# A hybrid decoder step: x tiles of blocks three to five transposed by DMA instead of by TensorE

## The chip, the cores and the metric

The kernel runs on the 8 cores of one Trainium2 chip. Every core does the same work on its own data: one prompt sequence of 2048 rows and 16 running sequences of 4 rows (64 sample rows). The cores don't talk to each other. The metric is the device time of the slowest core, in microseconds (us). In the text PE is TensorE, DVE is VectorE, ACT is ScalarE, POOL is GpSimd, and SP is the sync engine, which here only issues DMAs.

## The reference

```python
mod = silu(c) @ w_ada + b_ada                      # (B, 3D), D = 1024
shift, scale, gate = split(mod, 3)
h = rms_norm(x, g_norm) * (1 + scale) + shift
p = h @ w_in                                       # [h_A | B_A | C_A | z_A | u_B | v_B | z_B], 3584 wide
s = C_A * h_A
y_A = B_A * dwconv3(s) * silu(z_A)                 # width 512; a running sequence starts from its conv buffer
v_n = layer_norm(v_B, g_v, b_v)
y_B = u_B * (tril(W_s) v_n + b_s) * silu(z_B)      # width 512, chunks of 128 positions, 8 heads
out = rms_norm(x + gate * ([y_A | y_B] @ w_out), g_final)
```

Besides `out` for prompt and samples the kernel returns the conv buffers left behind and the normalised v rows of the samples.

## The kernel before

**Blocks.** The 16 tiles of 128 prompt rows are worked through in five blocks of 4, 4, 3, 3 and 2 tiles. The third block also holds the 64 sample rows as a fourth tile. In the code they have the indices 0 to 4 (`B.i`). A block needs `hT`, the modulated x with the 1024 features on the partitions, as 8 slices k of [128, rows]. There are two such buffers, block b uses `hT[b % 2]`.

**Preparing a tile.** `prep_load` loads 128 rows of x into `xa`; for the later blocks there are two such buffers. `prep_sq` takes the sum of squares on ACT (L378) and the power -1/2 on POOL (L380, L382). `prep_xn` scales the rows on DVE into `xn`, in bf16 (L389); there are two `xn` buffers. `prep2` transposes the tile on PE, as eight transpositions of 128x128 into one PSUM bank (L403), and copies the bank into `hT` on ACT (L408) or DVE (L410). When all tiles of the next block are there, `prep3` applies scale and shift in place, one slice k at a time, on ACT (L419) and DVE (L423, and L434, L437 for the sample columns).

**Working a block.** `A1(B, j)` and `A2(B, j)`, for j = 0 to 3, make four projections of group A (L477 on PE, with ACT and DVE reading the banks). `V` makes the projection of v and its statistics. `GB(B, j)` makes two projections of group B, takes a silu on ACT (L644), multiplies on DVE (L647), does the spatial mix on PE (L656), adds the bias on DVE (L666) and multiplies on POOL (L676). Between the calls of `GB` stands the output stage of the block before: `C_mm` is the output projection (L704), `C_s1` multiplies by the gate (L720, L721) and adds x on DVE (L723), `C_sq` takes the sum of squares on ACT (L733), `C_s2` makes the factor (L791, L793), and `C_s3` scales on DVE (L802) and stores.

**Where the preparation stands.** For blocks one and two it is worked in with the start-up and with block one. For block three (`PB[2]`) it is spread over block two: scaling of tiles 0 and 1 at `V` (j = 2), their transpositions at j = 3, those of tiles 2 and 3 (the samples) in `GB(0)` and `GB(1)`. For blocks four and five the scaling of tile 0 stands in `GB(3)` two blocks ahead, and the transposition of tile j behind `A2(B, j)` of the block before.

**Order.** Each engine and each DMA queue runs its instructions in the order in which the Python code emits them. `Sched.op` collects what an instruction must wait for from the names of the buffers that it reads and writes. Same-engine waits between two PE instructions are left out, but one between two DMAs never is, even if both stand in the same queue:

```python
if (not d.is_dma) and (not dma) and d.eng == eng:
    if eng == "pe":
        continue
    ...
o.deps.append(d)
```

A waiting DMA holds all that stands behind it in its queue. SP's queue holds the xa loads of the later blocks, the xc loads (x again, for the residual), the gate copies and all stores. PSUM has 8 banks, given out in turn by `nbank()`; a matmul waits until the last readers of its bank are done.

Of the kernel before, what the change touches and what calls it, by code (L numbers as in the profile page):

```python
# [5 lines left out]
F32 = mybir.dt.float32  # L6
# [6 lines left out]
D = 1024  # L13
# [177 lines left out]
def build_nc(limit=None):  # L191
# [42 lines left out]
    wout_bf = A("wout_bf", [128, 2, 8, 512], BF16)  # L234
    hT = [A(f"hT{i}", [128, 8, 512], BF16) for i in range(2)]
    NXA = 2
    xa = [A(f"xa{i}", [128, D], F32) for i in range(NXA)]
    xn = [A(f"xn{i}", [128, D], BF16) for i in range(2)]
    junk = A("junk", [128, D], BF16)
    spad = [A(f"spad{j}", [128, 514], F32) for j in range(4)]  # L240
    ssamp = [A(f"ssamp{j}", [128, 16, 6], F32) for j in range(4)]
    gv_bc = A("gv_bc", [64, 512], F32)
    bv_bc = A("bv_bc", [64, 512], F32)
    gf_bc = A("gf_bc", [128, D], F32)
    gate_p = A("gate_p", [128, D], F32)
    gate_s = A("gate_s", [128, D], F32)
    bsT = A("bsT", [128, 4, 128], F32)
    bias2 = A("bias2", [128, 4, 128], F32)
    Wt = A("Wt", [128, 8, 128], BF16)
# [122 lines left out]
    def prep_sq(B, i):  # L372
        ti, P, kind = B.tiles[i]
        ra = pst[(B.i, i)]
        rn = nxt("xn", 2)
        st, sres = nstat()
        ss, rs = st[0:P, 0:1], st[0:P, 1:2]
        op("act", lambda e: e.activation(out=junk[0:P, :], in_=xa[ra][0:P, :], func=AF.Square, accum_out=ss),  # L378
           r=[("xa", ra)], w=[sres, "junk"])
        op("pool", lambda e: e.tensor_scalar(out=rs, in0=ss, scalar1=1.0 / D, scalar2=EPS, op0=ALU.mult, op1=ALU.add),  # L380
           r=[sres], w=[sres])
        op("pool", lambda e: e.tensor_tensor(out=rs, in0=rs, in1=mhalf[0:P, 0:1], op=ALU.pow),  # L382
           r=[sres, "mhalf"], w=[sres])
        pst[(B.i, i)] = (ra, rn, rs, sres)

    def prep_xn(B, i):
        ti, P, kind = B.tiles[i]
        ra, rn, rs, sres = pst[(B.i, i)]
        op("dve", lambda e: e.tensor_scalar(out=xn[rn][0:P, :], in0=xa[ra][0:P, :], scalar1=rs, scalar2=None,  # L389
                                            op0=ALU.mult),  # L390
           r=[("xa", ra), sres], w=[("xn", rn)])
        pst[(B.i, i)] = rn

    def prep2(B, i, eng):
        ti, P, kind = B.tiles[i]
# [186 lines left out]
    def V_group(B, kind, grp, mid):  # L582
# [35 lines left out]
        def scale_v():  # L618
            for q, (ti, _) in enumerate(grp):
                bk = bks[q]  # L620
                if kind == "p":
                    op("act", lambda e, bk=bk, ti=ti, q=q: e.activation(  # L622
                        out=vn_bf[ti][:, :], in_=bk.t[:, :], func=AF.Identity, bias=nm[:, q:q + 1], scale=rs[:, q:q + 1]),
                       r=[bk.res, sres], w=[("vn", ti)])
                    continue
                vz, vzr = ntmp()
                op("act", lambda e: e.activation(out=vz[0:P, :], in_=bk.t[0:P, :], func=AF.Identity, bias=nm, scale=rs),
                   r=[bk.res, sres], w=[vzr])
                op("act", lambda e: e.copy(out=vn_s[:, :], in_=vz[0:P, :]), r=[vzr], w=["vn_s"])
                op("pool", lambda e: e.tensor_tensor(out=vnS[:, :], in0=vz[0:P, :], in1=gv_bc[:, :], op=ALU.mult),  # L630
                   r=[vzr, "gv_bc"], w=["vnS"])
                op("pool", lambda e: e.tensor_tensor(out=vnS[:, :], in0=vnS[:, :], in1=bv_bc[:, :], op=ALU.add),
                   r=["vnS", "bv_bc"], w=["vnS"])
                store(nvs[:, :], vnS[:, :], ["vnS"], "out_nvs")
        return scale_v
# [303 lines left out]
    def late_loads_2(g):  # L939
        load("sp", gate_p[:], bada_g.partition_broadcast(128), "bg_p", g)  # L940
        load("sp", gf_bc[:], g_final.partition_broadcast(128), "gf_bc", g)
        load("sp", gv_bc[:], g_v.partition_broadcast(64), "gv_bc", g)
        load("sp", bv_bc[:], b_v.partition_broadcast(64), "bv_bc", g)

    nb = len(PB)
    cq = []

    def C_step(B, i, nload=None):
        C_mm(B, i, 0, 8)
        C_s1(B, i)  # L950
        cq.append((B, i))
        if nload is not None:
            C_load(*nload)
        if len(cq) >= 3:
            C_s3(*cq.pop(0))
        if len(cq) >= 2:
            C_s2(*cq[-2])
# [5 lines left out]
    for b in range(nb):  # L963
# [15 lines left out]
        for j in range(4):  # L979
            if not late:  # L980
                if j < 2:
                    nxp(prep_load, j + 2)
            A1(B, j)
            if b == 0 and j == 3:
                V2()
            if not late:
                nxp(prep_sq, j + 1)
            elif j == 3 and b == 1:
                nxp(prep_sq, 2)
                nxp(prep2, 0, "act")  # L990
            if j < 2 and cq and not last:
                C_s3(*cq.pop(0))
                if cq:
                    C_s2(*cq[0])
            A2(B, j)
            if last and j == 2 and cq:
                C_s3(*cq.pop(0))
                if cq:
                    C_s2(*cq[0])
            if not late:  # L1000
                nxp(prep2, j, "act")
                nxp(prep_xn, j + 1)
            if b == 0 and j == 0:
                late_loads_1([("spadB", 0)])
            if b == 1 and j == 0:
                wblk_ops()
            if j == 2 and b > 1:
                first_c()
            if b == 1 and j == 2:
                nxp(prep_sq, 0)  # L1010
                nxp(prep_sq, 1)
            if j == (1 if last else 2):
                V(B, (lambda: nxp(prep_xn, 0)) if b == 1 else None)
                if b > 0:
                    V2()
            if b == 0 and j == 2:
                wt_ops()
            if b == 0 and j == 3:
                nxp(prep_sq, 0)
                nxp(prep_sq, 1)  # L1020
                bias2_ops()
                nxp(prep_xn, 0)
                nxp(prep_xn, 1)
            if b == 1 and j == 2:
                nxp(prep_xn, 1)
                nxp(prep_load, 2)
                nxp(prep_load, 3)
            if b == 1 and j == 3:
                nxp(prep2, 1, "act")
                nxp(prep_xn, 2)  # L1030
        if not late and N2 is not None:
            for i in range(2):
# [10 lines left out]
        for j in range(4):  # L1043
# [18 lines left out]
            if b == 1 and j >= 2:  # L1062
                prep3(NX, range(4 * j - 8, 4 * j - 4), "both")
            if j == 3 and N2 is not None and b > 0:
                prep_xn(N2, 0)
            GB(B, j)
            if b == 0 and j == 1:
                nxp(prep2, 0, "act")
                nxp(prep2, 1, "dve")
# [6 lines left out]
                nxp(prep2, 3, "dve")  # L1076
                prep3(NX, range(8), "both")
            if b == 1 and j < 2:
                nxp(prep2, 2 + j, "act")
                if j == 0:  # L1080
                    nxp(prep_xn, 3)
                prep_load(N2, j)
# [4 lines left out]
        if b == 0:  # L1087
            for k in range(8):
                S.alias(("yT", 1, k), [("wada", 3), ("xa", 6), ("xa", 7)])
            late_loads_2([("win", 22, 0)])  # L1090
        if last:
            C_mm(B, 0, 0, 7)
            C_mm(B, 0, 7, 8)
# [68 lines left out]
```

How the kernel before makes its waits and increments, by code:

```python
        def run(e, eng):  # L113
            seen = {}
            nw = 0
            for o in streams[e]:
                need = {}
                waits = list(o.deps)
                if o.is_dma and o.prev is not None:
                    waits.append(o.prev)
                for d in waits:
                    key = d.sem.num
                    if key not in need or need[key][1] < d.val:
                        need[key] = (d.sem, d.val)
                for key, (sem, val) in need.items():
                    if seen.get(key, 0) >= val:
                        continue
                    eng.wait_ge(sem, val)
                    seen[key] = val
                    nw += 1
                ins = o.fn(eng)
                if o.is_dma:
                    ins.then_inc(o.sem, 16)
                elif o.needed:
                    ins.then_inc(o.sem, 1)
            stats[e] = (len(streams[e]), nw)
# [18 lines left out]
            @block.sync  # L155
            def _(eng):
                run("sp", eng)
                for q in self.QUEUES:
                    last = {}
                    for o in streams[q]:
                        if o.is_dma:
                            last[o.sem.num] = (o.sem, o.val)
                    for sem, val in last.values():
                        eng.wait_ge(sem, val)
```

## Time and profile before

| | |
|---|---|
| median of 3 runs | 343.68 us (343.39 to 365.61) |
| the profiled execution | 343.48 us |
| its span, first to last instruction, slowest core | 341.7 us |
| spans of the 8 cores | 338.1 to 341.7 us |
| busy in the span: PE, DVE, ACT, POOL | 287.9, 186.5, 122.0, 110.6 us |
| granted PE clock, mean of the core | 0.970 |

The profile is of one execution on the slowest core. A timeline row gives the start and the duration of a merged group of instructions, and in brackets how long its engine had been idle before it and what ended that. Matmuls are pipelined, so the duration of a group of them overlaps the next group; distances between starts tell what PE spends. Block two runs from about 104 to 169 us, block three to 231, block four to 284, block five to the end.

### The profile page before, as it was taken

The page shows a single profiled execution, that of the slowest core. Times are in us where ns is not written, and L with a number is a line of the kernel's source. Part 1 is how long each engine was busy: PE and PEld are TensorE (multiplying, and loading weights), DVE is VectorE, ACT ScalarE, POOL GpSimd, SP SyncE. Part 2 cuts the span into 40 slices and gives each one's busy share as a digit, 9 for nine tenths or more (in the row PEclk, how much of TensorE's full clock was granted, in tenths as well). Part 3 has the DMA queues.
Part 4 walks back from the last instruction along what each step waited for, and adds up shares of the span by engine and source line. Part 5 has one row for each costly group of instructions (what it writes and reads, how often), then busy time and mean ns, then how long its engine had stood idle before and what let it go on. Part 6 is the DMA issues. An engine that isn't in the chain of part 4 may idle for free.

```text
span 341.7 us, 5602 instructions; the slowest of 8 cores (338.1 to 341.7 us)
## 1 busy us (share of the span) xinstructions
PE 287.9 (84%) x1767; PEld 151.4 (44%) x1792; DVE 186.5 (55%) x350; ACT 122.0 (36%) x215; POOL 110.6 (32%) x161
## 2 busy tenths in 40 slices
PE   0324639997799999999999999999999999999840
PEld 0222324443444445444455454446555557765410
DVE  0321015444564454846778836468863666667982
ACT  2611024207452234723445262443415244232320
POOL 7293065214423431412226342121432112222210
PEclk9999959999999999999999999999999999999995
DMA  5999999999999973193122715111180102527223
GB/s 130 214 166 165 170 160 146 176 160 257 204 213 182 228 131 94 31 255 118 62 92 93 205 44 149 61 63 62 61 238 11 33 0 94 154 70 195 90 111 124
DMA packets 14157, 44.51 MB, mean 130 GB/s; under 512 B 1968, under 2 KB 2352, under 8 KB 13104
## 3 DMA queue, kind: packets, MB, share of 16 engines
q0 software_dynamic: 6624, 21.24, 34.7%
q1 hardware_dynamic: 7504, 22.91, 22.2%
q8 instruction: 15, 0.25, 0.3%
q14 instruction: 14, 0.11, 0.1%
HBM read 51.02 MB, written 8.85 MB: 175 GB/s over the span
## 4 chain that ended last, share of the span: by engine, by line
PE 54%; DMA 24%; DVE 9%; issue 6%; POOL 3%; ACT 2%; DVEq 1%; POOLq 0%; SPq 0%; ACTq 0%
PE pb L477 31%; PE pb L704 12%; DMA win_bf<-win_l 12%; DMA wada<-wada_l 10%; PE pb L592 7%; DMA xc<-x_p 2%; DVE ob L802 2%; PE pb L403 2%; PE pb L656 1%; PE pb L814 1%; POOL xa L314 1%; DVE ob L723 1%; DVE tmp L532 1%; DVE ob L720 1%; DVE ob L721 1%
## 5 line engine op out<-in xcount | busy, mean ns | idle before, releaser
L477 PE MATMUL pb<-hT,win_bf 128*128 128x512 bf16 (+3 forms) x672 | 125.6, 341 | 4.1 <-DVE hT L410 1.8
L477 PEld LDWEIGHTS pb<-hT,win_bf 128*128 128x128 bf16 x680 | 66.0, 98 | 59.1 <-issue 4.9
L704 PE MATMUL pb<-wout_bf,yT 128*128 128x512 bf16 (+1 forms) x246 | 56.8, 379 | 2.7 <-POOL yT L676 1.2
L477 PE MATMUL pb<-hT,wh 128*128 128x512 bf16 (+3 forms) x277 | 53.9, 355 | 3.6 <-ACT hT L419 3.6
L676 POOL TENSOR_TENSOR yT<-tmp,tmp 128x512 bf16<-128x512 f32 (+3 forms) x20 | 22.0, 1098 | 67.7 <-DVE tmp L666 37.0
L551 POOL TENSOR_TENSOR yT<-tmp,tmp 128x512 bf16<-128x512 f32 (+3 forms) x20 | 23.7, 1185 | 58.0 <-DVE tmp L546 41.1
L733 ACT ACTIVATE junk<-ob 128x1024 bf16<-128x1024 f32 (+1 forms) x16 | 16.9, 1057 | 71.5 <-DVE ob L723 58.7
L477 PEld LDWEIGHTS pb<-hT,wh 128*128 128x128 bf16 x280 | 27.7, 100 | 27.9 <-issue 7.9
L532 DVE SCALAR_TENSOR_TENSOR tmp<-spad,pv,tmp 128x512 f32<-128x512 f32 (+2 forms) x40 | 26.3, 658 | 20.3 <-ACT tmp L525 13.1
L704 PEld LDWEIGHTS pb<-wout_bf,yT 128*128 128x128 bf16 (+1 forms) x256 | 23.9, 98 | 29.3 <-issue 2.4
L592 PE MATMUL pb<-wv_bf,hT 128*128 128x512 bf16 (+1 forms) x133 | 29.6, 379 | 0.2
L419 ACT ACTIVATE hT<-hT,shT,aT 128x384 bf16<-128x384 bf16 (+2 forms) x28 | 18.0, 694 | 26.3 <-DVE aT L468 25.4
L525 ACT ACTIVATE tmp<-spad,pv 128x512 f32<-128x512 f32 (+2 forms) x20 | 12.7, 636 | 38.4 <-DVE spad L514 29.7
L389 DVE TENSOR_SCALAR xn<-xa,stat 128x1024 bf16<-128x1024 f32 (+1 forms) x17 | 12.8, 755 | 24.5 <-POOL stat L382 24.4
L403 PE MATMUL pb<-ident,xn 128*128 128x128 bf16 (+1 forms) x136 | 11.5, 238 | 16.9 <-DVE xn L389 16.9
L514 DVE TENSOR_TENSOR spad<-pb,tmp 128x512 f32<-128x512 f32 (+2 forms) x20 | 11.7, 585 | 22.5 <-PE pb L477 11.0
L647 DVE TENSOR_TENSOR tmp<-pb,tmp 128x512 f32<-128x512 f32 (+3 forms) x20 | 11.9, 595 | 19.7 <-ACT tmp L644 19.7
L802 DVE SCALAR_TENSOR_TENSOR ob<-ob,stat,gf_bc 128x1024 f32<-128x1024 f32 (+1 forms) x16 | 20.5, 1280 | 1.5 <-POOL stat L793 1.4
L723 DVE TENSOR_TENSOR ob<-ob,xc 128x1024 f32<-128x1024 f32 (+1 forms) x15 | 18.4, 1225 | 4.7 <-DMA xc<-x_p 2.4
L378 ACT ACTIVATE junk<-xa 128x1024 bf16<-128x1024 f32 (+1 forms) x17 | 17.9, 1053 | 7.4 <-DMA xa<-x_p 7.0
L592 PEld LDWEIGHTS pb<-wv_bf,hT 128*128 128x128 bf16 (+1 forms) x136 | 13.3, 99 | 15.6 <-issue 0.4
L622 ACT ACTIVATE vn_bf<-pb,stat 128x512 bf16<-128x512 f32 x16 | 11.2, 774 | 24.2 <-DVE stat L616 12.8
(88 smaller groups left out, 261.1 us busy)
## 6 DMA issues: line engine op xcount, KB each, us to landing
y_p<-ob SPq DMA_DIRECT2D x15, 512.0 KB, 2.7
xc<-x_p SPq DMA_DIRECT2D x14, 512.0 KB, 7.8
wada<-wada_l POOLq DMA_DIRECT2D x6, 1024.0 KB, 36.0
xa<-x_p POOLq DMA_DIRECT2D x10, 512.0 KB, 40.1
win_bf<-win_l POOLq DMA_DIRECT2D x17, 256.0 KB, 43.5
xa<-x_p SPq DMA_DIRECT2D x8, 512.0 KB, 6.6
wout_bf<-wout_l POOLq DMA_DIRECT2D x2, 1024.0 KB, 60.4
wh<-winh_l POOLq DMA_DIRECT2D x4, 256.0 KB, 27.5
```

The lines of the kernel that those rows point to most:

```text
L378: op("act", lambda e: e.activation(out=junk[0:P, :], in_=xa[ra][0:P, :], func=AF.Square, accum_out=ss), r=[("xa", ra)], w=[sres, "junk"])
L403: ii = pe.transpose(out=tv[:, k, 0:P], in_=xn[rn][0:P, k * 128:(k + 1) * 128], identity=ident[0:P, 0:P])
L419: op("act", lambda e, k=k: e.activation(out=hb[:, k, 0:B.NP], in_=hb[:, k, 0:B.NP], func=AF.Identity, scale=aT[:, k, 0:1], bias=shT[:, k, ...
L477: ii = pe.matmul(bk.t[:, 0:B.N], lhsT=wsl(m, k), rhs=hT[B.h][:, k, 0:B.N], start=(k == 0), stop=(k == 7))
L532: ii = e.scalar_tensor_tensor(out=o[:, 0:NP], in0=spad[j][:, tp:tp + NP], scalar=cw(j, tp), in1=a[:, 0:NP], op0=ALU.mult, op1=ALU.add)
L551: op("pool", lambda e: e.tensor_tensor(out=yT[B.y][:, j, 0:N], in0=c2[:, 0:N], in1=sg[:, 0:N], op=ALU.mult), r=[c2r, sgr], w=[("yT", B.y, j)])
L592: ii = pe.matmul(bk.t[0:P, :], lhsT=hT[B.h][:, k, ti * 128:ti * 128 + P], rhs=wv_bf[:, k, :], start=(k == 0), stop=(k == 7))
L676: op("pool", lambda e: e.tensor_tensor(out=yT[B.y][:, 4 + j, 0:N], in0=tU[:, 0:N], in1=mb[:, 0:N], op=ALU.mult), r=[tUr, mbr], w=[("yT", B ...
L704: ii = pe.matmul(bk.t[R, :], lhsT=yT[B.y][:, k, ti * 128:ti * 128 + P], rhs=wout_bf[:, n, k, :], start=(k == 0), stop=(k == 7))
L723: op("dve", lambda e: e.tensor_tensor(out=o[R, :], in0=o[R, :], in1=xt[R, :], op=ALU.add), r=[ores, xr], w=[ores])
L733: op("act", lambda e: e.activation(out=junk[R, :], in_=o[R, :], func=AF.Square, accum_out=st[R, 0:1]), r=[ores], w=[sres, "junk"])
L802: op("dve", lambda e: e.scalar_tensor_tensor(out=o[R, :], in0=o[R, :], scalar=rs, in1=gf_bc[R, :], op0=ALU.mult, op1=ALU.mult), r=[ores, s ...
```

## The change

Nine tiles, those of blocks three to five, are no longer transposed by PE and copied by ACT. `prep_xn` issues a transposing DMA on SP right behind the scaling, from `xn` into `hT`. Tile 0 of blocks four and five goes into a buffer that the current block is still reading; its DMA (`prep2d`) is issued behind the last `GB` of that block. There are four `xn` buffers instead of two. Room for them comes from `gv_bc` and `bv_bc`, which move into the partitions 0 to 63 of `gate_s`, of which only 64 to 127 were used. Apart from this, `C_sq` of the output stage is now emitted in the following `GB`, behind its silu on ACT, instead of directly behind `C_s1`; `flush` does that, and once more behind the last `GB`.

```diff
+    NXN = 4
-    xn = [A(f"xn{i}", [128, D], BF16) for i in range(2)]
+    xn = [A(f"xn{i}", [128, D], BF16) for i in range(NXN)]
-    gv_bc = A("gv_bc", [64, 512], F32)
-    bv_bc = A("bv_bc", [64, 512], F32)
+    gv_bc, bv_bc = gate_s[0:64, 0:512], gate_s[0:64, 512:1024]
...
-    def prep_xn(B, i):
+    def prep_xn(B, i, now=True):
...
         pst[(B.i, i)] = rn
+        if B.i > 1 and now:
+            prep2d(B, i)
+
+    def prep2d(B, i):
+        ti, P, kind = B.tiles[i]
+        rn = pst[(B.i, i)]
+        dst = hT[B.h][:, :, ti * 128:ti * 128 + P]
+        op("sp", lambda e: e.dma_start(out=dst, in_=xn[rn][0:P, :], transpose=True),
+           r=[("xn", rn)], w=[("hT", B.h, i)] + [("hTk", B.h, k) for k in range(8)], dma=True)
...
+    sqp = []
+
+    def flush():
+        while sqp:
+            C_sq(*sqp.pop(0))
 
     def C_step(B, i, nload=None):
         C_mm(B, i, 0, 8)
-        C_s1(B, i)
+        C_s1(B, i, False)
+        sqp.append((B, i))
         cq.append((B, i))
...
             elif j == 3 and b == 1:
                 nxp(prep_sq, 2)
-                nxp(prep2, 0, "act")
...
             if not late:
-                nxp(prep2, j, "act")
                 nxp(prep_xn, j + 1)
...
             if b == 1 and j == 3:
-                nxp(prep2, 1, "act")
                 nxp(prep_xn, 2)
...
             if j == 3 and N2 is not None and b > 0:
-                prep_xn(N2, 0)
-            GB(B, j)
+                prep_xn(N2, 0, False)
+            GB(B, j, flush)
...
             if b == 1 and j < 2:
-                nxp(prep2, 2 + j, "act")
                 if j == 0:
                     nxp(prep_xn, 3)
...
+        flush()
+        if N2 is not None and b > 0:
+            prep2d(N2, 0)
```

## Rows read from the trace of the kernel before

**Rows 1.** The page: its first line, and the slices of PE and its clock.
```profile
span 341.7 us, 5602 instructions; the slowest of 8 cores (338.1 to 341.7 us)
...
PE   0324639997799999999999999999999999999840
...
PEclk9999959999999999999999999999999999999995
```
**Rows 2.** Waits of PE: line, who ended them, us in total, times, longest.
```profile
PE pb L403 <- DVE xn L389: 16.9, 6, 11.8
...
PE pb L477 <- DVE hT L410: 1.8, 1, 1.8
```
**Rows 3.** Timeline of PE, 90 to 342: start, us, line, count, idle before.
```profile
131.65 0.61 PE L403 MATMUL pb<-ident,xn 128*128 128x128 bf16 x8
132.10 3.62 PE L477 MATMUL pb<-hT,win_bf 128*128 128x512 bf16 x16
...
147.26 3.62 PE L477 MATMUL pb<-hT,win_bf 128*128 128x512 bf16 x16
...
158.84 3.63 PE L704 MATMUL pb<-wout_bf,yT 128*128 128x512 bf16 x16
...
189.07 0.61 PE L403 MATMUL pb<-ident,xn 128*128 128x128 bf16 x8 [0.19 <-DVE xn L389]
...
242.29 0.61 PE L403 MATMUL pb<-ident,xn 128*128 128x128 bf16 x8 [0.50 <-DVE xn L389]
242.73 5.36 PE L477 MATMUL pb<-hT,win_bf 128*128 128x384 bf16 x32
```
**Rows 4.** Groups by form: the copy out of PSUM on ACT.
```profile
L408 ACT COPY hT<-pb 128x1024 bf16<-128x1024 bf16 x12 | 12.1, 1005 | 5.5 <-PE pb L403 5.5
```
**Rows 5.** Waits of all engines, 85 to 342.
```profile
ACT junk L733 <- DVE ob L723: 58.7, 13, 6.3
```
**Rows 6.** Timeline of all engines, 150 to 200.
```profile
150.00 1.23 DVE L723 TENSOR_TENSOR ob<-ob,xc 128x1024 f32<-128x1024 f32 x1 [0.77 <-DMA xc<-x_p]
...
151.37 1.06 ACT L733 ACTIVATE junk<-ob 128x1024 bf16<-128x1024 f32 x1 [6.24 <-DVE ob L723]
...
153.10 0.69 DVE L647 TENSOR_TENSOR tmp<-pb,tmp 128x512 f32<-128x512 f32 x1 [1.88 <-ACT tmp L644]
...
169.10 0.43 DVE L437 TENSOR_TENSOR hT<-tmp,shT 128x256 bf16<-128x256 f32 x1 [1.67 <-ACT hT L419]
...
169.66 6.22 PE L477 MATMUL pb<-hT,wh 128*128 128x448 bf16 x32
...
175.87 0.34 SPq L314 DMA_DIRECT2D xa<-x_p  x1
```
**Rows 7.** DMA issues: queue, count, KB each, median us to landing.
```profile
xa<-x_s SPq DMA_DIRECT2D x1, 256.0 KB, 3.5
gate_p<-gate_p SPq DMA_DIRECT2D x2, 128.0 KB, 2.2
```
**Rows 8.** DMA queues, 135 to 139: packets, MB, share of 16 engines.
```profile
q1 hardware_dynamic: 4, 0.00, 0.5%
```
**Rows 9.** Timeline of all engines, 120 to 150.
```profile
130.63 0.33 SPq L314 DMA_DIRECT2D xa<-x_p  x1
...
132.47 0.47 SPq L314 DMA_DIRECT2D xa<-x_s  x1
...
136.58 1.04 ACT L378 ACTIVATE junk<-xa 128x1024 bf16<-128x1024 f32 x1
...
138.51 0.60 ACT L550 ACTIVATE tmp<-pb 128x512 f32<-128x512 f32 x1
...
143.84 1.29 SPq L314 DMA_DIRECT2D xc<-x_p  x3
```
**Rows 10.** Stretches: us, busy of PE, PEld, DVE, ACT, POOL, PEclk, DMA.
```profile
136.00:140.00 4.00, 3.95 (x21) 1.85 (x20) 2.95 (x4) 4.00 (x7) 1.72 (x3) 1.00 0.00 0
...
180.00:190.00 10.00, 9.76 (x63) 5.33 (x63) 8.68 (x15) 4.03 (x8) 6.47 (x6) 1.00 0.29 111
```

More of the change, by code:

```diff
@@ L374, in prep_sq @@
         ra = pst[(B.i, i)]
-        rn = nxt("xn", 2)
+        rn = nxt("xn", NXN)
         st, sres = nstat()
@@ L629, in scale_v @@
                 op("act", lambda e: e.copy(out=vn_s[:, :], in_=vz[0:P, :]), r=[vzr], w=["vn_s"])
-                op("pool", lambda e: e.tensor_tensor(out=vnS[:, :], in0=vz[0:P, :], in1=gv_bc[:, :], op=ALU.mult),
+                op("pool", lambda e: e.tensor_tensor(out=vnS[:, :], in0=vz[0:P, :], in1=gv_bc, op=ALU.mult),
                    r=[vzr, "gv_bc"], w=["vnS"])
-                op("pool", lambda e: e.tensor_tensor(out=vnS[:, :], in0=vnS[:, :], in1=bv_bc[:, :], op=ALU.add),
+                op("pool", lambda e: e.tensor_tensor(out=vnS[:, :], in0=vnS[:, :], in1=bv_bc, op=ALU.add),
                    r=["vnS", "bv_bc"], w=["vnS"])
@@ L941, in late_loads_2 @@
         load("sp", gf_bc[:], g_final.partition_broadcast(128), "gf_bc", g)
-        load("sp", gv_bc[:], g_v.partition_broadcast(64), "gv_bc", g)
-        load("sp", bv_bc[:], b_v.partition_broadcast(64), "bv_bc", g)
+        load("sp", gv_bc, g_v.partition_broadcast(64), "gv_bc", g)
+        load("sp", bv_bc, b_v.partition_broadcast(64), "bv_bc", g)
     nb = len(PB)
     cq = []
+    sqp = []
+    def flush():
+        while sqp:
+            C_sq(*sqp.pop(0))
     def C_step(B, i, nload=None):
         C_mm(B, i, 0, 8)
-        C_s1(B, i)
+        C_s1(B, i, False)
+        sqp.append((B, i))
         cq.append((B, i))
```

## The prediction

> **What bounds the kernel now.** I read the page's slices first: PE shows 9 tenths in every one from the twelfth of the 40 slices until the last three, at a granted clock of 9 tenths or more, which is the 2.4 GHz level [rows 1]. So from about 94 us on the kernel runs at PE's pace, and an edit there is worth what it takes out of PE's queue, as long as no other engine falls behind. The waits of PE confirm it: its largest item, 16.9 us for the xn tiles, has one wait of 11.8 us and belongs nearly all to the start-up, where the edited blocks are not yet at work [rows 2]. The next thing to read is PE's own timeline around each transposition that goes, and then the SP, ACT and DVE timelines of the second block (128 to 170 us), because there the new DMAs enter a queue that feeds the kernel.
>
> **What leaves PE.** Eight full tiles and the sample tile of blocks three to five are transposed by PE after 130 us. The price of one is the distance from its first transposition to PE's next group: 131.65 to 132.10 is 0.45 us, and the last, 242.29 to 242.73, is 0.44 us [rows 3]. The nine distances in order of time (the fourth is the sample tile's) are 0.45, 0.45, 0.45, 0.34, 0.44, 0.44, 0.66, 0.45 and 0.44: 4.12 us. Before two of them PE sat idle for the scaling, 0.19 and 0.50 us [rows 3]; those waits go too, since PE no longer reads xn. Sum: 4.8 us off PE. One matmul record there shows some 220 ns, but eight of them pass in 0.45 us, 56 ns apiece, since they are pipelined; the pitch is the price. The Trainium skill (TensorE: Matmul & The Clock Gate, "Part 4: PE-mode transpose") gives about 275 ns for one transposition in a kernel's context. Taken as a price each, the 72 would be worth 19.8 us; the rows speak for a latency and against this reading.
>
> **What leaves ACT.** Nine copies out of PSUM of about 1.0 us (the sample's is smaller) [rows 4], some 8.6 us in all. ACT is not late in these blocks, so I count nothing. The freed PSUM bank per tile only lengthens the distance until a bank is used again: nothing, or a little slack.
>
> **C_sq moved behind the next silu.** ACT waited 58.7 us in this way for DVE's L723 [rows 5], with the next prep3 and silu queued behind. In the second block that shows: C_sq at 151.37 held the silu, and DVE's L647 started at 153.10, 1.88 us late [rows 6]. Now L647 can follow L723 directly. PE did not wait for any of it, so the gain on the path is nothing; it is slack that I use below.
>
> **The other edits.** gv_bc and bv_bc in the lower half of gate_s: different partitions from those that the gates write, the same loads and the same two POOL operations, 0. Four xn buffers: the scaling no longer waits for the transposition of two tiles before; 0 on PE's path, as DVE's order stays.
>
> **What the DMAs cost.** No row shows a transposing DMA. Call L its time from issue to landing. Each moves 256 KB. The nearest rows: a sample load of the same nominal size lands in 3.5 us, a copy from SBUF to SBUF of half that in 2.2 us [rows 7]. As lower end I take 2.2. For the upper end: a transposition reads rows of 128 elements, 256 bytes, 1024 of them, 64 on each of 16 DMA engines; four small packets took 0.5% of 16 engines in 4 us, 80 ns each [rows 8]; 64 of them are 5.1 us, and with 2.2 us of fixed cost L is 7.3 us. I take 4 us, next to the row of the same size. The Trainium skill (DMA: Bandwidth & Descriptors, "Latency and other measured facts") gives 261 GB/s for a transposing DMA; 256 KB would move in an estimated 1.0 us and L would be near 3, which no run here shows yet.
>
> **Where the DMAs stand in SP's queue.** Five of the nine have time: block four's and block five's tiles are wanted by prep3 in the GB stage, over 10 us after the last of them is issued, and the one load that stands right behind such a transposition (175.87 before [rows 6]) is read nearly 9 us later. The critical place is the second block. prep2d writes hTk for all eight k, so each transposition must wait until the one before on the same hT has landed: Sched.op makes every DMA wait for a DMA that wrote the same name. There the order on SP is now T0, T1, load of tile 2, load of the sample tile. Before, the two loads went at 130.63 and 132.47 [rows 9]. Now T0 goes at 130.6, T1 waits for it until 130.6 + L, and both loads stand behind T1. So the tile-2 load goes out about L + 0.4 us later. Before, it had landed by 136, since no DMA is busy after that [rows 10], and its Square ran at 136.58 [rows 9].
> With L = 4 the Square starts at about 141 instead of 136.6. Behind it on ACT stand the silu of 138.51 and GB(0)'s; behind it in DVE stand the scaling of tile 2, the gate sums, and from these on SP the gate copies and the three xc loads (143.84 before) [rows 9]. All of it comes about L + 1 = 5 us later, so L723, 150.00 before [rows 6], starts near 155 and L647 of GB(1) near 156.3. Who waits? PE takes a bank again after eight others. The silu's bank is wanted at 147.26 less three removed tiles, 145.9 [rows 3]: the silu is done by 143. L647's bank is wanted by C_mm(2) at 158.84 less the four of this block, that is 157.1 [rows 3]; L647 without the wait for C_sq was due to end at 151.23 + 0.69 = 151.9, so a delay of 5.2 us is covered. L = 4 just fits: stall 0. The sample tile's T3 goes near 149 and lands near 154, ahead of prep3 at 158. For the end of the block, the last modulation ended at 169.5 just before PE wanted it at 169.66 [rows 6]; PE now comes at 168, but ACT's half no longer stands behind C_sq, and I expect it at 168.3, where the k that it frees is wanted at 168.7: 0, with 0.4 us to spare.
>
> **Sum.** 343.48 us of the profiled execution (span 341.7 and 1.8 around it) less 4.8 is 338.7; the median of the runs is 0.2 above the profiled one: 338.9.
>
> **Rivals.**
> (a) Partly hidden: L between 5 and 7. At 6 the delay is 7 against a cover of 5.2, so 1.8 us of stall at C_mm(2): 340.7; up to 343.7 at 7. For it: the small packets. Against: the load of the same size.
> (b) Slower, by SP's queue: from L = 7 on. At 7.3 C_mm(2) stalls 3.1 us, and T3, which waits for T2, makes prep3 of the second block about 2.4 later again: 5.5, so 338.9 + 5.5 = 344.4. Each further us costs some 2.5, as T0, T2 and T3 stand one behind the other in this chain: L = 10 gives about 351. So the change loses from L = 7 on, and by over 2% at L = 10. Against: no load in the trace has such a time unless others are queued with it.
> (c) DVE takes over where PE gets faster: 180 to 190 us has DVE at 8.68 of 10 us [rows 10]. Then the five tiles of blocks four and five (2.4 us and the 0.7 of waits) give nothing: 342.0. Against: it has 1.3 us to spare there, and PE wants at most 0.9 us of it, two removed tiles.
> (d) More than counted: PE's leftover waits, such as 1.8 us for L410 at 92 us [rows 2], shrink with ACT's and DVE's relief: up to 3 us more, 336. Against: they lie in block one, which keeps its PE transpositions. The skill's price per transposition as told above would give 323.7; I keep 0.02 for it.
>
> **Chances.** Forecast (337 to 341) 0.50; (a) 0.18; (b) 0.16, 0.12 of it beyond 2%; (c) 0.08; (d) 0.08 with the 0.02. A measurement of this kernel tells about 2% from no change. Faster by over 2% means under 336.8: part of (d) and 0.04 of the forecast's own spread, 0.11. Slower by over 2% (over 350.6) 0.13; within 2% 0.76. The range runs from 335.5, past most of (d), to 348.0, L = 8.7, which leaves out the worst of (b) and little else.
>
> **What would show it.** In the new trace: no L403 on PE after 100 us; PE's groups at 131.65 and 175.72 following each other with no gap; T1's issue on SP exactly at T0's landing, with the tile-2 load behind it and the Square about 4.5 us later; L647 without its 1.88 us of wait; no new wait of PE between 145 and 170 us. L itself stands in the DMA issues. The prediction is wrong if L is above 5, if a transposition holds the DMA engines so that the xc loads land late, or if PE shows waits for banks after 170 us.

## The result

The changed kernel takes 340.23 us in the median of its runs (339.12 to 341.0). Against runs of the kernel before on the same chip the ratio is 0.9889, with a 95% interval of 0.986 to 0.9918; of the 343.68 us before that is 3.8 us, 2.8 to 4.8. The forecast was 338.9 us, 4.8 us less than before. Ratios leave out executions in which the cores of a die ran at a lower clock and took several per cent longer, such as that of 365.61 us. Differences in us below are differences of ratios, taken of 343.7 us.

The page of the profile after, its first line and the slices of PE and its clock [rows 1]:

```profile
span 337.3 us, 5476 instructions; the slowest of 8 cores (334.1 to 337.3 us)
...
PE   0325539999899999998989999999999999999840
...
PEclk9999858999999999999999999999999999999995
```

The shape is that of before, 4.4 us shorter. Two slices behind 100 us show 8 tenths instead of 9, the 19th (152 to 160 us) in the second block and the 21st (169 to 177 us) at the start of block three. The waits of PE say what is new (lines as in [rows 2]; L403 is now L412, L477 is L486, L704 is L713, L647 is L656, L437 is L446):

```profile
PE pb L412 <- DVE xn L389: 16.0, 4, 11.6
...
PE pb L713 <- POOL yT L685: 1.2, 1, 1.2
PE pb L486 <- DVE hT L446: 1.1, 1, 1.1
PE pb L713 <- DVE tmp L656: 0.9, 1, 0.9
```

The wait for L389 has 4 items instead of 6: the two before transpositions of tiles of blocks four and five are gone. New are 1.1 us for L446, the last modulation of block three, and 0.9 us for L656, the multiplication behind the silu in GB(1). PE's timeline puts them in their places; these are the rows that answer to [rows 3] and to the end of [rows 6]:

```profile
127.01 7.07 PE L486 MATMUL pb<-hT,win_bf 128*128 128x512 bf16 x31
133.92 3.62 PE L823 MATMUL pb<-wada,lgx 128*128 128x512 bf16 x16
...
156.93 3.61 PE L713 MATMUL pb<-wout_bf,yT 128*128 128x512 bf16 x15 [0.87 <-DVE tmp L656]
...
167.74 0.92 PE L486 MATMUL pb<-hT,wh 128*128 128x448 bf16 x4
169.77 10.00 PE L486 MATMUL pb<-hT,wh 128*128 128x448 bf16 x52 [1.11 <-DVE hT L446]
```

The projections of 127.01 run on without a gap into L823 at 133.92, where two transpositions stood before. C_mm(2) of the second block starts at 156.93 after 0.87 us of idle time. Block three's first matmuls start at 167.74 and stop after the four slices k that are ready; the rest goes on at 169.77, after 1.11 us. From there to the end PE has no wait over 0.2 us that it did not have before.

**The ledger by PE's starts.** The v stage of block two began 1.19 us earlier in this execution (120.10 instead of 121.29), ahead of the first transposing DMA. Block three began 1.92 us earlier (167.74), its v stage 2.35 (187.38), block five's first output 3.89 (299.94), the last output 4.29 (321.29). So the second block gave 0.7 us, and block three up to its v stage 0.4 us, since the wait of 1.11 us took most of what the three transpositions there had cost. In all, PE was rid of 4.1 us of work and 0.7 us of waits and got 2.0 us of new waits, one late in the second block and one at the start of block three. The 1.19 us belong to the start-up: in the profiles of the kernels below whose first block is the same but for the number of xn buffers, this stage begins anywhere between 119.6 and 124.0 us.

What a transposing DMA takes stands in the DMA issues [rows 7]:

```profile
gate_p<-gate_p SPq DMA_DIRECT2D x2, 128.0 KB, 4.0
...
hT<-xn SPq DMA_TRANSPOSE x9, 3.2
```

L is 3.2 us in the median of nine, from 3.0 to 9.3. The chain of the second block, from the timeline of all engines (L723 is now L732, L419 is L428, L423 is L432), beside [rows 9] and the first rows of [rows 6]:

```profile
129.55 4.53 SPq L400 DMA_TRANSPOSE hT<-xn  x2
...
134.28 0.43 SPq L314 DMA_DIRECT2D xa<-x_p  x1
...
134.91 0.48 SPq L314 DMA_DIRECT2D xa<-x_s  x1
...
140.92 1.06 ACT L378 ACTIVATE junk<-xa 128x1024 bf16<-128x1024 f32 x1 [5.45 <-DMA xa<-x_p]
...
143.22 1.68 DVE L389 TENSOR_SCALAR xn<-xa,stat 128x1024 bf16<-128x1024 f32 x1 [5.22 <-POOL stat L382]
...
148.75 2.34 SPq L314 DMA_DIRECT2D xc<-x_p  x3
...
151.30 1.57 SPq L400 DMA_TRANSPOSE hT<-xn  x1
151.67 0.69 DVE L729 TENSOR_TENSOR ob<-pb,gate_p 128x512 f32<-128x512 f32 x1 [2.01 <-DMA gate_p<-gate_p]
...
154.85 1.23 DVE L732 TENSOR_TENSOR ob<-ob,xc 128x1024 f32<-128x1024 f32 x1 [1.89 <-DMA xc<-x_p]
...
155.99 0.68 DVE L656 TENSOR_TENSOR tmp<-pb,tmp 128x512 f32<-128x512 f32 x1
...
160.67 1.31 ACT L428 ACTIVATE hT<-hT,shT,aT 128x384 bf16<-128x384 bf16 x2 [3.30 <-DMA hT<-xn]
160.68 0.67 DVE L432 TENSOR_SCALAR hT<-hT,aT,shT 128x384 bf16<-128x384 bf16 x2 [0.70 <-DMA hT<-xn]
...
169.19 0.42 DVE L446 TENSOR_TENSOR hT<-tmp,shT 128x256 bf16<-128x256 f32 x1 [0.53 <-DVE tmp L443]
```

Read it down. T0 goes at 129.55, T1 only after T0 has landed, both together hold SP for 4.53 us. The load of tile 2 goes at 134.28, where it would have gone at 129.44 (130.63 less the 1.19 of the start-up): 4.8 us late. ACT sits idle for 5.45 us until it has landed, DVE for 5.22 until the scaling can run, the xc loads go at 148.75, L732 starts at 154.85 after 1.89 us of waiting for the first of them, and L656 follows at 155.99. PE wants that bank at 156.06 and gets it at 156.93. T3, the sample tile's transposition, is issued at 151.30 behind three xc loads of 512 KB in the same queue and lands 9.3 us later; ACT had then been idle for 3.30 us and DVE for 0.70 us.

The late issue is not all of the delay at the Square. The DMA issues give the landing time of the tile-2 load, before and after:

```profile
xa<-x_p SPq DMA_DIRECT2D x1, 512.0 KB, 3.4
...
xa<-x_p SPq DMA_DIRECT2D x1, 512.0 KB, 6.5
```

Before, it had landed by 134.0, and the Square of 136.58 came 2.5 us after that, in ACT's order behind other work. So the Square's delay against the v stage, 5.5 us (140.92 instead of 135.39), is, to 0.1 us, 4.8 us of later issue and 3.1 us of slower landing, less these 2.5 us.

### The profile page after: what moved, and what is told of

The parts are those of the page before. It is cut to its first block, busy times and chain, and to the rows that moved or that the text cites. A ratio compares the mean times of both kernels' runs of the same rounds, so it can differ in the third digit from the quotient of the medians.

```text
span 337.3 us, 5476 instructions; the slowest of 8 cores (334.1 to 337.3 us)
## 1 busy us (share of the span) xinstructions
PE 284.2 (84%) x1696; PEld 147.6 (44%) x1720; DVE 187.7 (56%) x350; ACT 114.1 (34%) x206; POOL 110.7 (33%) x161
## 4 chain that ended last, share of the span: by engine, by line
PE 42%; DMA 29%; DVE 12%; issue 7%; ACT 3%; POOL 3%; SPq 1%; DVEq 1%; POOLq 0%; ACTq 0%
PE pb L486 26%; DMA win_bf<-win_l 12%; DMA wada<-wada_l 11%; PE pb L713 8%; PE pb L601 4%; DVE ob L811 3%; DMA xa<-x_p 2%; DMA xc<-x_p 2%; DVE tmp L541 2%; DVE st L616 1%; PE pb L823 1%; ACT tmp L534 1%; POOL xa L314 1%; DVE ob L729 1%; DVE ob L730 1%
## 5 line engine op out<-in xcount | busy, mean ns | idle before, releaser
L486 PE MATMUL pb<-hT,win_bf 128*128 128x512 bf16 (+3 forms) x672 | 125.1, 341 | 2.0 <-DMA win_bf<-win_l 1.4
L486 PEld LDWEIGHTS pb<-hT,win_bf 128*128 128x128 bf16 x680 | 66.0, 98 | 57.5 <-issue 2.7
L713 PE MATMUL pb<-wout_bf,yT 128*128 128x512 bf16 (+1 forms) x246 | 56.6, 379 | 3.4 <-POOL yT L685 1.2
L486 PE MATMUL pb<-hT,wh 128*128 128x512 bf16 (+3 forms) x277 | 54.0, 356 | 4.7 <-ACT hT L428 3.6
L486 PEld LDWEIGHTS pb<-hT,wh 128*128 128x128 bf16 x280 | 27.8, 100 | 29.7 <-issue 9.8
L713 PEld LDWEIGHTS pb<-wout_bf,yT 128*128 128x128 bf16 (+1 forms) x256 | 23.9, 98 | 29.9 <-issue 2.9
L389 DVE TENSOR_SCALAR xn<-xa,stat 128x1024 bf16<-128x1024 f32 (+1 forms) x17 | 13.7, 806 | 27.4 <-POOL stat L382 27.4
L428 ACT ACTIVATE hT<-hT,shT,aT 128x384 bf16<-128x384 bf16 (+2 forms) x28 | 18.0, 695 | 29.4 <-DVE aT L477 25.2
L653 ACT ACTIVATE tmp<-pb 128x512 f32<-128x512 f32 (+3 forms) x20 | 10.3, 514 | 37.2 <-PE pb L486 37.2
L802 POOL TENSOR_TENSOR stat<-stat,mhalf 128x1 f32<-128x1 f32 x16 | 9.5, 596 | 37.2 <-DVE stat L800 24.5
L732 DVE TENSOR_TENSOR ob<-ob,xc 128x1024 f32<-128x1024 f32 (+1 forms) x15 | 18.4, 1225 | 5.6 <-DMA xc<-x_p 3.3
L412 PE MATMUL pb<-ident,xn 128*128 128x128 bf16 x64 | 6.3, 263 | 16.0 <-DVE xn L389 16.0
```

What stands on the lines that cost most here:

```text
L428: op("act", lambda e, k=k: e.activation(out=hb[:, k, 0:B.NP], in_=hb[:, k, 0:B.NP], func=AF.Identity, scale=aT[:, k, 0:1], bias=shT[:, k, ...
L486: ii = pe.matmul(bk.t[:, 0:B.N], lhsT=wsl(m, k), rhs=hT[B.h][:, k, 0:B.N], start=(k == 0), stop=(k == 7))
L713: ii = pe.matmul(bk.t[R, :], lhsT=yT[B.y][:, k, ti * 128:ti * 128 + P], rhs=wout_bf[:, n, k, :], start=(k == 0), stop=(k == 7))
L732: op("dve", lambda e: e.tensor_tensor(out=o[R, :], in0=o[R, :], in1=xt[R, :], op=ALU.add), r=[ores, xr], w=[ores])
```

## The experiments

Every kernel was timed beside the kernel before; ratios are to that.

**Block three's tiles back on PE.** The transpositions of block three return to their old places; the DMA keeps five tiles.

```diff
+    PE3 = (0, 1, 2, 3)
...
-        if B.i > 1 and now:
+        if (B.i > 2 or (B.i == 2 and i not in PE3)) and now:
...
+                nxp(prep2, 0, "act")
...
+                nxp(prep2, 1, "act")
...
+                if True:
+                    nxp(prep2, 2 + j, "act")
```

> Block three's four tiles go back to PE at their old places; the five tiles of blocks four and five stay on the DMA, and the rest of the change stays. Theory Q (in the second block the new DMAs in SP's queue hold the loads and so cost PE its 0.87 and 1.11 us of new waits, which eats the 1.7 us that the four tiles give): time equal to the changed kernel's within 0.5 us, ratio to before 0.989 to 0.991, and no wait of PE over 0.3 us between 140 and 172 us. Rival D (those waits come from the pace of DVE and ACT in that block, not from the queue): they stay, and the time is 1.5 us above the changed kernel's, ratio about 0.994.

Measured: 0.9921 (0.9895 to 0.9948), 340.8 us. PE has no wait of over 0.3 us between 140 and 172 us. As the queue's theory wants, the new waits go with the DMAs of the second block. The time lies between the two forecasts and decides nothing: it is 1.1 us above the changed kernel's where 0.5 us at most was expected, and the intervals of both overlap. It says that the four tiles on the DMA were worth 1.1 us in the changed kernel, with zero inside the noise.

**No wait of one transposition for another.**

```diff
+    def war(B, i):
+        S.alias(("hTw", B.i, i), [("hTk", B.h, k) for k in range(8)])
+        return ("hTw", B.i, i)
...
-           r=[("xn", rn)], w=[("hT", B.h, i)] + [("hTk", B.h, k) for k in range(8)], dma=True)
+           r=[("xn", rn)], w=[("hT", B.h, i), war(B, i)], dma=True)
```

> As the changed kernel, but a transposition no longer waits for the one before on the same hT: each has a name of its own that takes over the readers of the old contents. Theory Q: the second transposition and both xa loads go out 1.5 us earlier, the wait at C_mm(2) falls from 0.87 to 0 and the one at block three's start from 1.11 to some 0.3; ratio to before about 0.985. Rival D: no change, 0.989. Rival R (what delays the loads is that a load behind a transposition starts only after its data, as the gap of 2 us between the last small packet and the first large one suggests): the loads are issued earlier and land at nearly the same time, ratio 0.988 to 0.989.

Measured: 0.9858 (0.9835 to 0.9882), 338.8 us: 1.1 us less than the changed kernel. Both new waits are gone. SP's timeline:

```profile
131.23 2.96 SPq L404 DMA_TRANSPOSE hT<-xn  x2
134.39 0.43 SPq L314 DMA_DIRECT2D xa<-x_p  x1
```

The two transpositions hold SP for 2.96 us instead of 4.53. The v stage began at 121.78 here, so counted from it the load goes 1.6 us earlier than in the changed kernel, and its Square, at 138.66, runs 3.9 us earlier. So 1.6 us come from the earlier issue and the other 2.3 from the landing: in the changed kernel 6.5 us after the issue, here 4.1. The changed kernel has 1.9 us without a packet, from 135.45 until 137.35, between T1's last small packets and the load's first large ones, though the load was issued at 134.28. These are its GB/s from 135 to 137 and from 137 to 139 us, in 40 slices each, and then those of this kernel from 135 to 137, where the large packets follow at 135.45 without a gap:

```profile
GB/s 215 195 184 190 205 139 77 41 11 0 0 0 0 0 0 0 0 0 0 0 0 0 0 0 0 0 0 0 0 0 0 0 0 0 0 0 0 0 0 0
...
GB/s 0 0 0 0 0 0 0 82 0 82 82 0 82 246 82 0 0 164 82 164 492 164 410 573 82 410 573 246 410 573 246 410 492 246 410 246 655 164 328 737
...
GB/s 195 266 179 189 195 205 154 261 150 400 272 256 164 164 164 0 0 0 0 0 0 246 492 410 164 0 82 410 410 82 410 655 0 82 1065 164 82 819 328 82
```

Rival R forecast that the gap stays and eats the earlier issue; its ratio and its landing did not come. But the gap that it starts from is real in the changed kernel, and it went with the wait between the transpositions. In the four kernels in which a transposition that waits for another stands ahead of the load, the load took 5.3 to 6.9 us to land; in the kernel before and in the seven others in which none stands ahead of it, 3.4 to 5.2. What holds it is not shown.

**The loads first.**

```diff
-                V(B, (lambda: nxp(prep_xn, 0)) if b == 1 else None)
+                V(B, (lambda: nxp(prep_xn, 0, False)) if b == 1 else None)
...
-                nxp(prep_xn, 1)
                 nxp(prep_load, 2)
+                nxp(prep_xn, 1, False)
                 nxp(prep_load, 3)
+                nxp(prep2d, 0)
+                nxp(prep2d, 1)
```

> As the changed kernel, but in the second block the two xa loads stand ahead of the two transpositions on SP, each right behind the scaling that frees its buffer. Theory Q and rival R alike: the Square of tile 2 runs near 135.5 instead of 140.9, the gates and the xc loads come 5 us earlier, both new waits of PE go, 2.0 us less than the changed kernel, ratio to before about 0.983. Rival D: no change, 0.989.

Measured: 0.9848 (0.9823 to 0.9872), 338.3 us: 1.4 us less than the changed kernel, no wait of PE over 0.2 us between 100 and 300 us. The loads stand where they stood before, 9.3 and 11.2 us behind the start of the v stage at 119.60, and the transpositions behind them (a third is merged into the group; its 8.73 us hold waits of the queue):

```profile
128.93 0.33 SPq L314 DMA_DIRECT2D xa<-x_p  x1
130.77 0.47 SPq L314 DMA_DIRECT2D xa<-x_s  x1
131.39 8.73 SPq L400 DMA_TRANSPOSE hT<-xn  x3
```

The order of one queue was the whole of the two waits; DVE and ACT do the same work here (rival D is refuted). The interval of this ratio overlaps that of the changed kernel, as does that of the kernel before this one; what carries the reading is that both waits are gone in both traces, and in that of the next kernel. About 0.6 us of the expected 2.0 did not come: in this execution PE waits 1.0 us at the third output of the last block, for DVE behind a late xc load.

**Both mends.** The two edits together.

> Both mends of the second block's queue at once: the xa loads ahead of the transpositions, and no wait of one transposition for another. Each alone gave 0.985 to 0.986 and took away both new waits of PE. Theory Q: nothing is left to gain there, ratio to before 0.984 to 0.985 as for either alone. Rival: the two add up, 0.981.

Measured: 0.9852 (0.9834 to 0.9869), 338.2 us. They don't add up: either alone takes away both waits, and nothing was left to gain there.

**The squares back behind C_s1.**

```diff
-        C_s1(B, i, False)
-        sqp.append((B, i))
+        C_s1(B, i)
...
-            GB(B, j, flush)
+            GB(B, j)
```

> The changed kernel with C_sq back directly behind C_s1 on ACT. Theory Q with the cover of the prediction: in the second block the first xc load lands 5 us later than before, C_sq(0) then holds ACT's silu for another 1.2 us and L656 of GB(1) comes about 2 us later than in the changed kernel; the wait at C_mm(2), 0.87 us there, becomes 2 to 3 us. Ratio to before 0.994 to 0.996. Rival N (the place of C_sq doesn't matter, ACT has room): 0.989 as the changed kernel.

Measured: 0.9997 (0.9973 to 1.0021), 343.6 us, more than the 0.994 to 0.996 that were expected. Without the moved squares the transposing DMAs gain nothing. The mechanism is the expected one, from the timeline of that kernel:

```profile
153.81 1.23 DVE L732 TENSOR_TENSOR ob<-ob,xc 128x1024 f32<-128x1024 f32 x1 [0.17 <-DVE ob L730]
...
155.18 1.06 ACT L742 ACTIVATE junk<-ob 128x1024 bf16<-128x1024 f32 x1 [10.99 <-DVE ob L732]
...
156.92 0.69 DVE L656 TENSOR_TENSOR tmp<-pb,tmp 128x512 f32<-128x512 f32 x1 [1.88 <-ACT tmp L653]
...
157.96 3.61 PE L713 MATMUL pb<-wout_bf,yT 128*128 128x512 bf16 x16 [1.67 <-DVE tmp L656]
```

The Square at 155.18 stands between L732 and the silu, L656 starts 1.88 us late, PE idles 1.67 us before C_mm(2). But 3.7 us were lost, and the two waits of PE explain 2.3 of them (1.67 and 2.61 against 0.87 and 1.11). The rest is in the clock. The stretches around the second wait (columns: length, busy PE, PEld, DVE, ACT, POOL, granted clock, DMA share, GB/s):

```profile
165.00:170.00 5.00, 4.68 (x29) 2.08 (x28) 4.83 (x9) 1.88 (x3) 1.82 (x2) 1.00 0.01 2
170.00:172.30 2.30, 0.01 (x1) 0.04 (x2) 0.53 (x3) 2.10 (x5) 0.74 (x2) 1.00 0.57 228
172.30:174.00 1.70, 1.70 (x7) 0.78 (x8) 1.70 (x3) 0.00 (x0) 0.00 (x0) 0.75 0.05 14
174.00:176.00 2.00, 2.00 (x7) 0.83 (x6) 1.83 (x4) 0.00 (x0) 1.27 (x1) 0.50 0.00 0
176.00:180.00 4.00, 4.00 (x21) 1.99 (x20) 2.89 (x6) 2.04 (x4) 0.55 (x1) 0.93 0.28 103
```

After 2.6 us in which PE did next to nothing, the granted clock was 0.75 and then 0.50, the 1.2 GHz level, until 176 and 1.00 again later: 0.25 of 1.7 us, 0.5 of 2 us and 0.07 of 4 us are 1.7 us of lost work. In the changed kernel, after 1.11 us of idle time at the same place, the clock stays at 1.00. The 2.3 us of waits and these 1.7 us are 4.0, near the 3.7 that were lost.

**The squares alone.** The kernel before with C_sq moved and nothing else.

> The kernel before with C_sq moved behind the next silu and nothing else. The kernel with everything but the DMAs gave 0.9973 (0.995 to 0.9996). Theory B (that gain of some 0.9 us is that of the four xn buffers: no wait of a scaling for the transposition two tiles earlier, so PE's waits of 0.19 and 0.50 us go): here 1.000, and those two waits of PE stay. Theory C (it is C_sq's place: ACT and DVE come earlier, in blocks three and four as well as in the last): here 0.997 as there, and the two waits of PE are gone.

Measured: 0.9979 (0.9955 to 1.0004), 343.0 us. PE has no wait for the scaling in blocks three and four in this profile, so the two of 0.19 and 0.50 us go without four xn buffers and without a DMA. But it has one of 1.5 us at the third output of the last block, for L647, that the kernel before has not. So what there is of a gain comes with the place of the squares, but the interval reaches 1.

**Everything but the DMAs.** The kernel before with four xn buffers, gv and bv in gate_s, and the moved squares.

> The kernel before with everything of the change but the transposing DMAs: four xn buffers, gv and bv in gate_s, squares behind the next silu. In the changed kernel's profile 1.2 us were already gained when the second block's v stage began, before any transposing DMA. Theory X (the four buffers took a wait out of block one): 1.2 us less than before, ratio 0.9965. Rival S (the start-up's weight loads ended earlier in that execution by chance): ratio 1.000.

Measured: 0.9973 (0.995 to 0.9996), 343.3 us: 0.9 us, 0.1 to 1.7. Its v stage of block two began at 123.95, the latest of all: the four buffers do not bring the early start that the changed kernel's profile showed. What differs from the squares alone, 0.0006, can't be told from nothing.

**Two transpositions doubled, in the second block.** T0 and T1 are each issued twice, one behind the other.

```diff
+        if once and (B.i == 2 and i < 2):
+            prep2d(B, i, False)
```

> The changed kernel with the first two transposing DMAs of the second block (T0 and T1) issued twice, each waiting for the one before. A transposition lands 3.2 us after its issue, so the xa loads behind them go out some 6.4 us later. Theory Q: nearly all of it arrives at C_mm(2), the wait there grows from 0.87 to about 7 us, time 6 us above the changed kernel's, ratio to before 1.006 to 1.01. Rival D (queue has no part in the waits): 0.989. The slope of the prediction, 2.5 us of time for each us of L, would give more than 8 us here, as both transpositions are lengthened by 3.2 us.

Measured: 1.005 (1.0026 to 1.0075), 345.5 us: 5.5 us more than the changed kernel. The queue and PE's new waits in that kernel:

```profile
130.54 10.86 SPq L400 DMA_TRANSPOSE hT<-xn  x4
141.60 0.43 SPq L314 DMA_DIRECT2D xa<-x_p  x1
```

```profile
148.82 2.75 PE L488 MATMUL pb<-hT,win_bf 128*128 128x512 bf16 x8 [2.94 <-ACT tmp L561]
152.59 3.57 PE L488 MATMUL pb<-hT,win_bf 128*128 128x512 bf16 x8 [1.02 <-DVE gate_p L832]
```

The four hold SP for 10.86 us, and the load goes 6.3 us later than in the changed kernel (counted from the v stage, 1.0 us later here). The place of the stall was not the expected one: PE stops at 148.82 for the bank of the silu L561 and at 152.59 for that of a gate sum, 4.0 us in all, before C_mm(2) has its turn. The clock was 0.59 and 0.56 of full in the two stretches of 4 us behind that, 149 to 157. PE was busy for 2.98 and 4.00 us of them, so some 3.0 us of work were lost (0.41 of 2.98 and 0.44 of 4.00, an estimate); with 2.0 us more of waits than in the changed kernel this makes 5.0 of the 5.5 us.

**Five transpositions doubled, in the later blocks.** The same edit with `B.i > 2`.

> The changed kernel with the five transposing DMAs of blocks four and five issued twice. Each stands in SP's queue in front of loads and stores that have time. Theory Q (place decides, not the number or the time of the DMAs): no change against the changed kernel, ratio to before 0.989, no new wait of PE over 0.3 us after 172 us. Rival E (a transposing DMA costs through the DMA engines or SBUF, wherever it is issued): some 0.5 us for each, 2.5 us more, ratio 0.996.

Measured: 0.9877 (0.9844 to 0.991), 339.4 us: the same as the changed kernel. Five more transposing DMAs, some 16 us of landing time, cost nothing that the time shows, where what stands behind them has time. The expected picture was missed in one point: PE has two new waits in the last block, 0.68 us for L658 and 0.35 us for the silu L655. The kernel with both mends, which doubles nothing, has 0.87 and 0.35 us at the same two places.

**Early xc loads in the last block.**

```diff
         if last:
             for i in range(len(B.tiles)):
                 C_load(B, i, i)
+            first_c()
...
-            if j == 2 and b > 1:
+            if j == 2 and b > 1 and not last:
                 first_c()
```

> As the kernel with both mends, and in the last block the three xc loads stand at its start instead of behind a store that waits for DVE. In the profiles DVE waits 1.2 to 2.7 us there for the first xc load, and PE up to 1.0 us at the third output projection. If that wait is on the path, 0.5 to 1.0 us less, ratio about 0.982; if the last block is held by DVE's own work, the wait of DVE goes and the time stays at 0.984.

Measured, on top of both mends: 0.9812 (0.9792 to 0.9831), 336.8 us, 1.4 us less. It is the fastest kernel of the study. PE's wait for yT in the last block falls from 1.2 to 0.7 us, and those for L656 and L653 in the last block are gone.

> The kernel before with the early xc loads of the last block alone. The same two outcomes as for the early loads on top of the mends: 0.998 if the wait is on the path, 1.000 if not.

Measured, on the kernel before: 0.9965 (0.9953 to 0.9977), 342.2 us, 1.2 us less. It is independent of the change.

**Two tiles of block two on the DMA as well**, on top of the mends and the early xc loads.

```diff
-        if B.i > 1 and now:
+        if (B.i > 1 or (B.i == 1 and i < 2)) and now:
...
-                nxp(prep2, 0, "act")
-                nxp(prep2, 1, "dve")
```

> As the last, and tiles 0 and 1 of block two go to the DMA too. PE loses two transpositions (1.0 us) and its wait of up to 1.8 us for the copy on DVE; but the weight loads keep the DMA engines at 9 tenths until 95 us, so each transposition has to share them. If it lands within 8 us of the scaling, 1 us less than the last, ratio about 0.979. If it lands later, the second block's start waits and the time is that of the last or above it.

Measured: 1.0833 (1.0804 to 1.0863), 372.1 us, 35 us more than without it. SP's timeline, PE's waits, and the DMA queues between 100 and 110 us (packets, MB, share of 16 engines):

```profile
84.76 33.91 SPq L404 DMA_TRANSPOSE hT<-xn  x2
118.84 1.16 SPq L314 DMA_DIRECT2D gate_p<-bada_g  x1
```

```profile
PE pb L490 <- DVE hT L436: 33.6, 3, 30.8
```

```profile
q0 software_dynamic: 270, 1.83, 97.9%
q1 hardware_dynamic: 270, 0.07, 5.5%
```

The two transpositions landed 46 us after their issue. While POOL's queue (q0) still has weights to load, both queues get exactly as many packets, 270 each in these 10 us and 404 each in the 10 us before. One of q0's carries 6.8 KB, one of the transposition's 256 bytes, so the transposition gets 5.5% of the engines' time and PE waits 30.8 us for it.

## Why the prediction was right, and what it had wrong

**PE's share: right.** 4.12 us of transpositions and 0.69 us of waits leave PE. Where the new waits are removed (0.9858, 0.9848, 0.9852) the kernel gains 4.9 to 5.2 us; 0.1 to 1.7 us of that came without any DMA (0.9973). The 0.69 us of waits are in this part: they were put down to PE no longer reading xn, but they are gone in the kernel with the squares alone as well.

**The place of the danger: right.** T1 waited for T0 on SP, both loads stood behind it, and the chain through Square, scaling, gate sums and xc loads ended at L647's bank for C_mm(2), with 5.2 us of cover. L732 began 6.0 us late, and the wait was 0.87 us, near 6.0 less 5.2.

**L: 3.2 us where 4 was taken, and yet the delay was larger.** The forecast took the tile-2 load as L + 0.4 = 4.4 us late at L = 4; it was 4.8 us at L = 3.2, since T0 and T1 also take 1.3 us of SP's own time apiece, which the forecast had as that of a plain load. The delay of the Square came out for a reason that the forecast did not have. It let the load land by 136, 5.4 us after its issue, and so passed all of the later issue on to the Square. The load had landed after 3.4 us, at 134.0, and 2.5 us of the later issue would have cost nothing. The changed kernel's load took 6.5 us instead, 3.1 more, and this used them up. That the forecast's 5 us are so near to the 5.5 measured is luck: two omissions, of 2.5 and 3.1 us, against each other. "L = 4 just fits: stall 0" failed by what they leave and by the 0.4 us of later issue, and cost 0.9 us.

**The end of the second block: wrong, a wait of 1.1 us.** I had expected the last modulation at 168.3 and 0.4 us to spare; L446 ended at 169.6, in an execution that was 1.19 us ahead. T3 was to land near 154; the xc loads ahead of it in its queue were left out of its L, and it landed at 160.6. DVE and ACT waited for it, and DVE had hardly a gap from then until L446. With either mend T3 still takes 7.1 and 8.2 us to land, but some 6 us or more earlier against the v stage, and PE does not wait: the cost lay in the late start of the chain more than in T3's own time.

**C_sq: the value was too small.** "The gain on the path is nothing; it is slack that I use below" is right for the kernel before (0.9979, an interval that reaches 1). In the changed kernel it is worth 3.7 us, all that the change gains. I used the slack in the sum, but gave no price for its loss; and the price is larger than the waits, because the longer one brings the clock down.

**Rivals.** (a) was nearest to what happened: partly hidden, with 2.0 us of stall, though at an L of 3.2 and not of 5 to 7; its 340.7 us at L = 6 is nearer to the measured 340.23 than the forecast's 338.9. (b) is the doubled kernel's case: slower by 0.5% with T0 and T1 lengthened by 3.2 us each. The slope of 2.5 us for each us of L is not tested by it: T2 and T3, which the slope counts, kept their length, and T1 stood in front of the loads twice. What it shows is 5.5 us for loads that go 6.3 us later, some 0.9 us for each us. (c) did not come. DVE was busy for 8.74 of the 10 us from 180 to 190 [rows 10], and PE did not wait for it:

```profile
180.00:190.00 10.00, 9.95 (x52) 5.00 (x52) 8.74 (x15) 2.74 (x6) 6.54 (x6) 1.00 0.48 161
```

(d): the 1.8 us wait of block one is not in this profile, and 1.19 us were gained by the v stage of block two, but that stage's start varies by over 4 us among kernels with the same first block, so nothing of it can be put down to the change. The Trainium skill (TensorE: Matmul & The Clock Gate, "Part 4: PE-mode transpose") gives about 275 ns for one transposition in a kernel's context. Taken as a price in PE's queue this is refuted by the kernels without new waits: the 72 gave about 5 us, not 19.8. The Trainium skill's 261 GB/s for a transposing DMA (DMA: Bandwidth & Descriptors, "Latency and other measured facts") is above what this trace shows: T1's small packets came at 184 to 215 GB/s in the first five slices of the stretch from 135 us shown above. The L near 3 us that was worked out from it was the better estimate: 3.2 us were measured, 4 had been taken.

**Range and sign.** 340.23 us lies 1.3 above the forecast and inside 335.5 to 348.0; the ratio is inside the 2% that had 0.76. By its own signs the forecast failed in two points: it wanted no new wait of PE between 145 and 170 us, and there are two, and it wanted L at 5 us or below, where T3 took 9.3. The stalls that it had at nothing are 2.0 us, more than the 1.3 us by which the time is off; where the difference comes from is not shown, and the runs themselves lie between 339.12 and 341.0.

## What to carry to other kernels

Work moved from the bounding engine to a DMA queue costs what stands behind it in that queue: put the transfers that someone waits for in front, and look for a dependency by name that makes one DMA wait for another. Read when a transfer has landed, and not only when it was read: the distance between the two is slack. Price the cover as well as the edit: take it away on paper once, since an edit that "costs nothing beside it" may be what holds the gain. And before a transfer of small packets shares the engines with a bulk load of another queue, count packets and not bytes.

## What the runs showed of the hardware

- A transposing DMA of a [128, 1024] bf16 tile took 1.2 to 1.6 us of SP's issue time and once 2.8 (at 233.90 us in the changed kernel), 3.0 to 3.5 us to land when alone, and moved packets of 256 bytes at about 200 GB/s (131 to 132 us, 164 to 256 GB/s). Single plain issues took 0.33 to 0.71 us.
- Two queues moved equal numbers of packets, 404 to 404 and 270 to 270 in 10 us each: with a bulk load in the other queue, whose packets were of 6.8 KB in the second of these stretches, the same DMA took 46 us.
- In one queue the transposition came behind what was issued before it: 9.3 us behind three loads of 512 KB.
- A load of 512 KB behind a transposition that had waited for another landed after 5.3 to 6.9 us in four kernels, in one of them with 1.9 us without any packet; in eight others after 3.4 to 5.2. The reason is open.
- An idle time of PE of 2.6 us was followed by a granted clock of 0.75 to 0.50 for 3.7 us, and idle times of 2.9 and 1.0 us close together by 0.59 and 0.56 over 8 us; one of 1.1 us alone was not.
